# A decoder layer on one core: seven bodies with stops of their own, and constant waits on VectorE

## The chip, the core and the metric

One core of one Trainium2 chip. The engines are TensorE (PE; PEld is its weight load), VectorE (DVE), ScalarE (ACT), GpSimd (POOL) and SyncE (SP), which issues most DMAs. Time is the device time of one launch in microseconds (us); lower is better.

## What is computed

One layer of a decoder over 1024 tokens of width 1024, all in float32:

```python
x = x + hybrid_mixer(rmsnorm(x))            # MLA heads | gated linear recurrence | differential attention, then W_out
x = x + memory_cross_attention(rmsnorm(x))  # 256 memory rows, 4 heads
x = x + peer_ffn(rmsnorm(x))
return rmsnorm(x)

def peer_ffn(h):                            # 8 heads, 128 keys on each of two sides, 16 experts a head
    top_s, top_i = top_k(scores(h), 16)     # per side
    best_s, best_c = top_k(pairs_of(top_s), 16)
    experts = ...                           # 128 experts a token
    act = gelu(einsum('td,thkd->thk', h, u[experts]))
    return einsum('thk,thkd->td', softmax(best_s) * act, v[experts])
```

Each token needs 128 rows of `u` and 128 rows of `v`, 4 KB each, chosen by its own scores: 1.07 GB of gathered rows in all.

## The kernel before

The tokens are worked on in eight blocks of 128, one token to a partition. For a block the kernel has two kinds of work. The **rows**: 128 positions p, at each of which row p of `u` for every token is multiplied with the token's hidden vector and summed on VectorE (`multiply_row`, L2052), and a row of `v` is added to the result, thirteen positions later. Seven of eight `v` rows are summed on TensorE: ScalarE makes a diagonal matrix of the coefficients (L1528), and four matmul instructions add the row into PSUM (`add_row`, L1267). Each eighth is added on VectorE (L2074). The **front**: everything that leads from the block's x to its expert numbers and gates. Its pieces, in order, are `latents`, `mla_up`, `conv`, `gates`, `recur`, then attention (`mla_0` to `mla_3`, `diff_0` to `diff_3`, four heads each), `join`, `mix_out`, `norm_cross`, `cross_q`, `cross_scores`, `cross_mix`, `cross_out`, `norm_ffn`, `peer_q`, `peer_scores`, the top-16 searches (`top_0`, `choose_0`, `top_1`, `choose_1`), and, since the next block's first projection is drawn ahead, `next_square`, `next_norm`, `next_0` to `next_4`.

After an opening that prepares block 0 alone come seven **bodies**. Body n multiplies the rows of block n and runs the front of block n+1. A body is a loop that runs once, with its own number of key tiles for the attention (`LOOPS`: 2 in body 0 to 8 in body 6); body 6 has no next projection. At the end the rows of block 7 stand alone. The bodies' instruction streams are in order on each engine, and the order between rows and front is written out: `Pace.run` takes, for each piece of the front, a tuple of **stops** from the engine's table. A piece is cut into **parts** (`pace.part`), and before each part the engine first does all positions below the part's stop:

```python
            def part(self, share):

                self.to(int(self.first + share * (self.last - self.first)) if self.bp is None else next(self.ahead))
...
                        if self.bp is not None:
                            self.ahead = iter(self.stops[self.body][name])
```

So a part with stop 41 on TensorE starts when TensorE has been through positions 0 to 40. Parts with equal stops follow one another with no row between. TensorE, VectorE and ScalarE each have a table with one entry a body; all seven entries of a table are equal, but for the pieces that body 6 lacks. The parts wait for each other across engines by semaphores: a score matmul on TensorE (L1114, L1118), its masked maximum on VectorE (`masked_max`, L1834), the exponential on ScalarE (L1441), the transpose on TensorE in two halves (`turn_p`, L1100), between which ScalarE copies the first half out (`out_pT`), the values on TensorE (L1126).

GpSimd has no front. It issues the gathers (`retrieve`): one of `u`, one of `v`, in turn, 512 KB each, into two rings of nine rows. A `u` gather (L810) waits until VectorE has multiplied the row that held its slot; a `v` gather (L824) waits for the sum of the row that held its slot. `v` runs twelve rows behind `u`. SyncE loads weights in pairs of slices of 512 KB into a ring of four (`load_pair`); a pair is loaded when TensorE has used up the one four before. The weight pieces are `mix_out`, `cross_q`, `cross_out`, `peer_q` (eight pairs each) and `next_0` to `next_4` (17 pairs together).

VectorE counts three of its waits in registers: `wait_more` waits for a register's value plus n and then adds n to the register. It is used before each score maximum (twelve in a body), before each `top`, and between the steps of each top-16 search (`top16`): 32 times in a body.

## Time and profile before

| | us |
|---|---|
| median of 3 runs | 3484.84 |
| lowest and highest | 3477.87, 3487.18 |
| span of the profiled execution, first to last instruction (its own time; the page has no other) | 3488.4 |
| of it: opening, to the first row of body 0 | 306.6 |
| bodies 0 to 6, each from its first row product to the next body's | 384.3, 403.3, 401.5, 400.4, 413.2, 422.9, 412.2 |
| rows of block 7, end | 344.0 |

In the rows below, a window line gives the stretch in us from the span's start, its length, the busy time of each engine with the number of its instructions in brackets, the granted clock of TensorE as a share of full speed (2.4 GHz; the only other level is 1.2 GHz), the mean busy share of the 16 DMA engines, and the rate at which they moved data. A group line gives line, engine, operation, output and inputs, shapes and count, then busy time and the mean of one in ns, then the engine's idle time before it and what ended that. Busy time of TensorE is modelled from starts, since matmuls are pipelined.

### The profile page before, as it was taken

Reading aid. Unit: us, or ns where it says so; the run is one execution under the profiler, and the core shown is the slowest. Engines: PE = TensorE matmul, PEld = TensorE weight load, DVE = VectorE, ACT = ScalarE, POOL = GpSimd, SP = SyncE. Lnnn points to the kernel's source line nnn. Section 1 sums busy time; section 2 is a strip of 40 time slices with the busy share of each in tenths; the row PEclk is TensorE's granted clock in tenths of the full one; section 3 lists DMA queues with packets and bytes.
Section 4 is the critical chain, followed back from the end, with each engine's and each line's share of the span. In section 5 each row is a group of like instructions: output and inputs, shape, how many; then the busy total and the mean of one; then the engine's idle time right before and its main releaser. Section 6 shows DMA issues by size and latency. Waiting matters only on the chain.

```text
span 3488.4 us, 34790 instructions
## 1 busy us (share of the span) xinstructions
PE 2948.9 (85%) x10984; PEld 1651.9 (47%) x10984; DVE 2349.6 (67%) x5893; ACT 812.5 (23%) x1915; POOL 2015.7 (58%) x2085
## 2 busy tenths in 40 slices
PE   7876898888988898889997899888998889976675
PEld 6465455544545355534554456444564445522222
DVE  6229846886588765886578765886648865596555
ACT  3111411132211421133211322114221232211111
POOL 1004755666566765666565655665556655477775
PEclk9898999999999999999999999998999999999998
DMA  7788999999999999999999999999999999999998
GB/s 279 277 274 313 408 409 409 408 409 409 409 407 406 394 409 409 408 407 382 409 409 408 392 356 409 409 409 348 359 409 409 409 355 342 385 404 410 409 409 347
DMA packets 386971, 1345.09 MB, mean 386 GB/s; under 512 B 41762, under 2 KB 44834, under 8 KB 386148
## 3 DMA queue, kind: packets, MB, share of 16 engines
q0 software_dynamic: 294912, 1073.87, 78.1%
q1 hardware_dynamic: 90724, 264.79, 20.0%
q10 hardware_dynamic: 1152, 4.19, 0.3%
q8 instruction: 90, 1.47, 0.2%
q14 instruction: 93, 0.76, 0.1%
HBM read 1332.99 MB, written 35.39 MB: 392 GB/s over the span
## 4 chain that ended last, share of the span: by engine, by line
PE 38%; DMA 30%; DVE 15%; POOL 9%; issue 6%; ACT 3%; SPq 1%; DVEq 0%; POOLq 0%; ACTq 0%
PE ps_sum L1267 18%; DMA rows<-in_peer_u,ids_u 13%; DMA rows<-in_peer_v,ids_v 10%; PE ps_p L999 5%; POOL rows L824 5%; POOL rows L810 4%; DVE rows L2052 4%; PE ps_s L1181 4%; DMA rows<-in_peer_v,ids_u 3%; DMA w_ring<-packed 3%; PE ps_s L1118 2%; PE ps_p L1126 2%; DVE feat_b L1935 1%; DVE feat_b L1931 1%; PE ps_s L1114 1%
## 5 line engine op out<-in xcount | busy, mean ns | idle before, releaser
L1267 PE MATMUL ps_sum<-rows,diag 128*128 128x512 f32 x3548 | 1727.6, 629 | 267.1 <-DMA rows<-in_peer_v,ids_v 141.4
L2052 DVE CUSTOM_DVE_ANT_0 rows<-h_cur,rows 128x1024 f32<-128x1024 f32 x1024 | 1226.8, 1220 | 496.3 <-DMA rows<-in_peer_u,ids_u 483.3
L810 POOL DMA_INDIRECT rows<-in_peer_u,ids_u x1024 | 1012.3, 989 | 702.0 <-issue 483.3
L1267 PEld LDWEIGHTS ps_sum<-rows,diag 128*128 128x128 f32 x3548 | 671.0, 200 | 1155.7 <-issue 1005.7
L824 POOL DMA_INDIRECT rows<-in_peer_v,ids_v x512 | 490.3, 958 | 433.8 <-PE ps_sum L1267 277.6
L824 POOL DMA_INDIRECT rows<-in_peer_v,ids_u x512 | 498.2, 973 | 284.7 <-PE ps_sum L1267 144.2
L1528 ACT ACTIVATE diag<-ident,acts 128x128 f32<-128x128 f32 x887 | 324.7, 394 | 1049.4 <-PE ps_sum L1267 750.1
L999 PE MATMUL ps_p<-hT,w_ring 128*128 128x128 f32 x2944 | 358.7, 282 | 28.8 <-DMA w_ring<-packed 15.3
L999 PEld LDWEIGHTS ps_p<-hT,w_ring 128*128 128x128 f32 x2944 | 353.0, 198 | 61.2 <-issue 39.7
L1834 DVE CUSTOM_DVE_ANT_0 e<-ps_s,bias_t 128x256 f32<-128x256 f32 (+6 forms) x96 | 74.2, 773 | 176.3 <-PE ps_s L1118 73.7
L2074 DVE SCALAR_TENSOR_TENSOR x_cur<-rows,acts,x_cur 128x1024 f32<-128x1024 f32 x137 | 175.6, 1282 | 7.4 <-DMA rows<-in_peer_v,ids_v 7.3
L1905 DVE TENSOR_TENSOR x_next<-x_next,ps_s 128x512 f32<-128x512 f32 x32 | 21.9, 685 | 200.0 <-PE ps_s L1181 200.0
L1516 ACT ACTIVATE acts<-dots 128x8 f32<-128x8 f32 x128 | 26.6, 208 | 486.9 <-DVE dots L2052 486.6
L1181 PE MATMUL ps_s<-w_ring,hT 128*128 128x512 f32 x256 | 118.3, 608 | 14.2 <-DMA w_ring<-packed 7.4
L1441 ACT ACTIVATE e<-e,small 128x256 f32<-128x256 f32 (+6 forms) x96 | 75.4, 785 | 219.7 <-DVE small L1836 219.4
L999 PE MATMUL ps_p<-pT,w_ring 128*128 128x128 f32 x1024 | 118.8, 276 | 0.9 <-DMA w_ring<-packed 0.9
L999 PEld LDWEIGHTS ps_p<-pT,w_ring 128*128 128x128 f32 x1024 | 116.9, 192 | 5.4 <-issue 3.3
L1181 PE MATMUL ps_s<-w_ring,feat_b 128*128 128x512 f32 x256 | 114.8, 592 | 1.1 <-DMA w_ring<-in_wstream 1.1
L1935 DVE FIND_INDEX8 feat_b<-feat_b,e 128x8 uint32<-128x128 f32 (+1 forms) x384 | 103.4, 279 | 0.0
L1118 PE MATMUL ps_s<-k_diff,feat_a 32*128 32x512 f32 (+2 forms) x192 | 83.7, 543 | 16.9 <-DVE small L1836 16.8
L1314 ACT ACTIVATE feat_a<-ps_p 128x512 f32<-128x512 f32 (+2 forms) x48 | 26.0, 542 | 304.6 <-PE ps_p L999 304.5
L2052 DVE DVE_READ_ACCUMULATOR2_ANT dots<- 128x1 f32 x1024 | 84.4, 82 | 0.0
(288 smaller groups left out, 2376.2 us busy)
## 6 DMA issues: line engine op xcount, KB each, us to landing
w_ring<-packed SPq DMA_DIRECT2D x343, 512.0 KB
w_ring<-in_wstream SPq DMA_DIRECT2D x65, 512.0 KB
packed<-in_wstream SPq DMA_DIRECT2D x49, 512.0 KB, 8.2
rows<-in_peer_u,ids_u POOLq DMA_INDIRECT x1024, 14.9
rows<-in_peer_v,ids_u POOLq DMA_INDIRECT x512, 12.6
rows<-in_peer_v,ids_v POOLq DMA_INDIRECT x512, 19.3
bias_rows<-rows SPq DMA_DIRECT2D x5, 1024.0 KB, 12.1
bias_t<-in_x SPq DMA_DIRECT2D x8, 512.0 KB, 7.9
```

What stands on the lines that cost most here:

```text
L810: pool.indirect_dma_start(u_rows[:, slot, :], None, peer_u, bass.IndirectOffsetOnAxis(ap=ids_u[:, j:j + 1], axis=0)).then_inc(u_landed[slo ...
L824: pool.indirect_dma_start(v_rows[:, slot, :], None, peer_v, bass.IndirectOffsetOnAxis(ap=ids[:, j:j + 1], axis=0)).then_inc(v_landed[slot] ...
L999: ins = pe.matmul(dst, w[:, k, :], lhs[:, kt, :], start=(kt == 0), stop=(kt == KT - 1))
L1118: ins = pe.matmul(ps_s[:, c0:c1], q_diff[r:r + DK, half // 4, :], k_diff[r:r + DK, half // 4, c0:c1], start=True, stop=True)
L1181: pe.matmul(ps_s[:, n * 512:(n + 1) * 512], lhs[:, kt, :], w, start=(kt == 0), stop=(kt == KT - 1)).then_inc(w_used, 1)
L1267: ins = pe.matmul(ps_sum[:, c * 512:(c + 1) * 512], diag[:, n % 4, :], v_rows[:, slot, c * 512:(c + 1) * 512], start=(j == 0), stop=(n == ...
L1441: act.activation(buf[:, 0:keys_n], buf[:, 0:keys_n], ACT.Exp, bias=small[:, 32 + n:33 + n], accum_out=small[:, 48 + n:49 + n]).then_inc(s_ ...
L1528: act.activation(diag[:, n % 4, :], ident[:, :], ACT.Copy, scale=coef[:, j:j + 1]).then_inc(diag_made, 1)
L1834: run(dve.tensor_tensor_reduce(buf[:, 0:keys_n], ps_s[:, 0:keys_n], bias[:, 0:keys_n], 1.0, -3.0e38, ALU.add, ALU.max, small[:, 16 + n:17 ...
L1935: dve.max_index(i[:, first:first + 8], v[:, first:first + 8], s).then_inc(top_step, 1)
L2052: dve.tensor_tensor_reduce(row, h_cur[:, :], row, 1.0, 0.0, ALU.mult, ALU.add, dots[:, p:p + 1]).then_inc(u_used, 1)
L2074: dve.scalar_tensor_tensor(x_cur[:, :], v_rows[:, slot, :], coef[:, j:j + 1], x_cur[:, :], ALU.mult, ALU.add)\
```

## The change

Each of the seven entries of the three tables gets numbers of its own. `next_*` parts, `join`, attention, the searches and the rest keep their order; only the positions at which an engine turns to them differ. On VectorE the three counted waits no longer use registers: since each body runs once, the running count is known when the program is built, and `wait_for` waits for that constant. The waits, their number and their places are the same. SyncE's and GpSimd's programs don't change.

The diff, cut: of the old tables the entry that all bodies share; of TensorE's new one the lines for attention, join, `mix_out` and the end of each of bodies 0 to 6, body 6 in full; of VectorE's the lines of the searches, bodies 0 to 6 in order; of ScalarE's the entry of body 5.

```diff
 TENSOR_STOPS = [
-    {"latents": (1,), "mla_up": (9,), "gates": (17, 18), "recur": (20, 26), "mla_0": (29, 30, 31), "mla_1": (31, 31, 32),
-     "mla_2": (32, 33, 35), "mla_3": (35, 35, 37), "diff_0": (37, 38, 40, 41), "diff_1": (41, 43, 43, 44),
-     "diff_2": (45, 47, 48, 49), "diff_3": (49, 49, 51, 51), "join": (54, 56), "mix_out": (56, 56, 58, 58, 58),
-     "norm_cross": (59, 62), "cross_q": (62, 62, 62, 67, 67), "cross_scores": (69,), "cross_mix": (70, 73, 74),
-     "cross_out": (75, 75, 76, 78, 81), "norm_ffn": (83, 83), "peer_q": (83, 83, 85, 86, 88), "peer_scores": (89,),
-     "next_norm": (93, 99), "next_0": (104, 104, 106, 106), "next_1": (106, 106, 108, 108, 108),
-     "next_2": (112, 121, 121, 121, 121), "next_3": (121, 121, 124, 126, 126), "next_4": (126, 128, 128)},
...
+    {"latents": (8,), "mla_up": (16,), "gates": (19, 19), "recur": (23, 25), "mla_0": (27, 32, 32), "mla_1": (32, 32, 32),
+     "mla_2": (33, 33, 35), "mla_3": (35, 35, 35), "diff_0": (35, 40, 41, 41), "diff_1": (41, 42, 42, 42),
+     "diff_2": (42, 43, 47, 49), "diff_3": (49, 49, 49, 49), "join": (50, 53), "mix_out": (53, 59, 59, 63, 65),
...
+     "next_3": (108, 108, 108, 108, 108), "next_4": (108, 108, 114)},
+    {"latents": (4,), "mla_up": (12,), "gates": (18, 19), "recur": (19, 29), "mla_0": (32, 32, 32), "mla_1": (32, 33, 33),
+     "mla_2": (33, 34, 34), "mla_3": (34, 34, 34), "diff_0": (34, 42, 42, 42), "diff_1": (42, 43, 43, 44),
+     "diff_2": (48, 51, 51, 52), "diff_3": (52, 52, 52, 52), "join": (57, 62), "mix_out": (65, 65, 65, 65, 66),
...
+     "next_2": (104, 110, 110, 110, 110), "next_3": (110, 110, 110, 110, 114), "next_4": (114, 114, 114)},
+    {"latents": (0,), "mla_up": (1,), "gates": (7, 9), "recur": (22, 22), "mla_0": (24, 24, 26), "mla_1": (26, 26, 28),
+     "mla_2": (29, 30, 30), "mla_3": (30, 30, 31), "diff_0": (31, 33, 33, 36), "diff_1": (37, 42, 42, 42),
+     "diff_2": (43, 46, 46, 53), "diff_3": (53, 53, 53, 53), "join": (53, 56), "mix_out": (57, 57, 58, 58, 58),
...
+     "next_2": (107, 107, 107, 107, 108), "next_3": (108, 120, 120, 120, 120), "next_4": (120, 120, 120)},
+    {"latents": (3,), "mla_up": (4,), "gates": (8, 17), "recur": (24, 26), "mla_0": (28, 30, 31), "mla_1": (31, 31, 32),
+     "mla_2": (32, 34, 34), "mla_3": (37, 37, 37), "diff_0": (37, 41, 41, 41), "diff_1": (41, 44, 44, 44),
+     "diff_2": (46, 49, 49, 50), "diff_3": (50, 58, 58, 59), "join": (63, 63), "mix_out": (63, 63, 63, 63, 63),
...
+     "next_2": (105, 105, 105, 105, 108), "next_3": (110, 111, 111, 111, 111), "next_4": (111, 115, 115)},
+    {"latents": (3,), "mla_up": (3,), "gates": (7, 20), "recur": (22, 24), "mla_0": (29, 30, 30), "mla_1": (30, 31, 32),
+     "mla_2": (32, 32, 33), "mla_3": (33, 33, 35), "diff_0": (37, 38, 39, 40), "diff_1": (40, 42, 43, 43),
+     "diff_2": (45, 46, 49, 50), "diff_3": (50, 52, 62, 62), "join": (64, 65), "mix_out": (65, 65, 65, 66, 66),
...
+     "next_3": (108, 108, 108, 108, 108), "next_4": (108, 108, 108)},
+    {"latents": (3,), "mla_up": (9,), "gates": (19, 19), "recur": (19, 25), "mla_0": (28, 31, 31), "mla_1": (31, 32, 32),
+     "mla_2": (33, 34, 35), "mla_3": (35, 35, 38), "diff_0": (38, 39, 40, 41), "diff_1": (41, 43, 43, 44),
+     "diff_2": (44, 48, 48, 48), "diff_3": (48, 49, 51, 52), "join": (66, 66), "mix_out": (66, 66, 66, 66, 66),
...
+     "next_2": (104, 105, 105, 105, 105), "next_3": (109, 110, 111, 112, 112), "next_4": (112, 112, 113)},
+    {"latents": (2,), "mla_up": (2,), "gates": (7, 8), "recur": (8, 26), "mla_0": (28, 30, 30), "mla_1": (30, 31, 32),
+     "mla_2": (32, 33, 34), "mla_3": (34, 34, 38), "diff_0": (38, 39, 40, 41), "diff_1": (41, 43, 43, 44),
+     "diff_2": (45, 47, 48, 53), "diff_3": (53, 53, 57, 58), "join": (63, 64), "mix_out": (65, 65, 65, 65, 65),
+     "norm_cross": (66, 66), "cross_q": (67, 67, 67, 69, 70), "cross_scores": (71,), "cross_mix": (71, 79, 81),
+     "cross_out": (82, 83, 85, 85, 85), "norm_ffn": (88, 88), "peer_q": (90, 90, 90, 91, 92), "peer_scores": (92,)},
 ]
 VECTOR_STOPS = [
-    {"latents": (0, 6), "mla_up": (8,), "conv": (17,), "gates": (19, 19, 21, 23), "recur": (25, 26), "mla_0": (26,),
-     "mla_1": (29,), "mla_2": (33,), "mla_3": (39,), "diff_0": (39, 39, 39), "diff_1": (42, 42, 43), "diff_2": (43, 45, 48),
-     "diff_3": (50, 52, 52), "join": (53, 54), "mix_out": (54, 55, 57, 57), "norm_cross": (59, 59, 63), "cross_scores": (71,),
-     "cross_mix": (71, 72), "cross_out": (73, 76, 84, 84), "norm_ffn": (85, 85, 85), "next_square": (90, 93),
-     "top_0": (93, 94, 94, 94, 97, 99), "next_norm": (99, 103),
-     "choose_0": (104, 105, 105, 105, 106, 108, 108, 108, 108, 111, 111), "top_1": (113, 113, 113, 113, 114, 117),
-     "choose_1": (120, 120, 124, 125, 126, 126, 126, 128, 128, 128, 128)},
...
+     "top_0": (92, 92, 93, 94, 94, 97), "next_norm": (97, 97), "choose_0": (97, 97, 97, 97, 97, 98, 98, 99, 102, 107, 107),
+     "top_1": (107, 109, 109, 109, 109, 109), "choose_1": (109, 109, 109, 109, 111, 111, 115, 115, 116, 120, 121)},
...
+     "top_0": (95, 95, 95, 95, 95, 95), "next_norm": (95, 95), "choose_0": (95, 96, 96, 96, 97, 99, 99, 99, 111, 111, 112),
+     "top_1": (114, 114, 114, 114, 114, 114), "choose_1": (114, 114, 115, 115, 115, 115, 115, 115, 119, 119, 121)},
...
+     "top_0": (95, 96, 96, 96, 98, 100), "next_norm": (105, 105),
+     "choose_0": (105, 105, 105, 105, 105, 105, 106, 106, 106, 106, 106), "top_1": (106, 106, 106, 106, 106, 106),
+     "choose_1": (111, 121, 121, 121, 121, 121, 121, 121, 121, 121, 121)},
...
+     "top_0": (95, 98, 98, 98, 100, 101), "next_norm": (102, 102),
+     "choose_0": (105, 105, 105, 105, 105, 105, 105, 105, 105, 105, 106), "top_1": (112, 112, 112, 112, 112, 112),
+     "choose_1": (113, 114, 116, 116, 117, 117, 117, 119, 120, 127, 128)},
...
+     "top_0": (96, 97, 97, 97, 97, 97), "next_norm": (97, 97), "choose_0": (98, 98, 98, 99, 103, 103, 105, 105, 105, 105, 105),
+     "top_1": (105, 105, 105, 105, 109, 109), "choose_1": (109, 109, 109, 109, 109, 110, 114, 121, 121, 122, 123)},
...
+     "top_0": (91, 95, 99, 99, 99, 101), "next_norm": (102, 102),
+     "choose_0": (102, 102, 102, 102, 103, 103, 104, 104, 104, 109, 111), "top_1": (111, 111, 111, 111, 111, 111),
+     "choose_1": (111, 111, 111, 111, 112, 112, 112, 113, 113, 113, 117)},
...
+     "cross_mix": (77, 80), "cross_out": (80, 82, 86, 87), "norm_ffn": (87, 90, 90), "top_0": (93, 97, 97, 97, 97, 97),
+     "choose_0": (97, 103, 104, 104, 104, 104, 106, 108, 108, 110, 110), "top_1": (110, 110, 110, 112, 113, 113),
+     "choose_1": (113, 122, 127, 127, 127, 127, 127, 127, 128, 128, 128)},
 ]
 SCALAR_STOPS = [
-    {"latents": (1, 7), "mla_up": (10,), "gates": (14, 18, 20), "mla_0": (28, 30), "mla_1": (30, 30), "mla_2": (32, 32),
-     "mla_3": (32, 34), "diff_0": (34, 38, 42), "diff_1": (42, 42, 42), "diff_2": (47, 47, 48), "diff_3": (48, 51, 53),
-     "norm_cross": (59,), "cross_q": (59, 60, 67), "cross_scores": (71,), "cross_mix": (73, 73, 74), "norm_ffn": (82,),
-     "peer_q": (82, 84, 88), "next_square": (90,), "peer_scores": (90,), "next_0": (104, 109), "next_1": (114, 114),
-     "next_2": (117, 120), "next_4": (125, 125), "choose_1": (125, 125)},
...
+    {"latents": (4, 5), "mla_up": (6,), "gates": (6, 20, 20), "mla_0": (28, 30), "mla_1": (30, 30), "mla_2": (32, 32),
+     "mla_3": (32, 33), "diff_0": (36, 39, 40), "diff_1": (42, 43, 43), "diff_2": (44, 44, 47), "diff_3": (48, 50, 50),
+     "norm_cross": (71,), "cross_q": (71, 71, 71), "cross_scores": (72,), "cross_mix": (72, 72, 72), "norm_ffn": (86,),
+     "peer_q": (91, 91, 91), "next_square": (91,), "peer_scores": (91,), "next_0": (95, 100), "next_1": (101, 102),
+     "next_2": (104, 106), "next_4": (110, 111), "choose_1": (117, 117)},
...
 ]
             steps = Steps(dve_step)
-            scores_waited, keys_waited, top_waited = (counter(dve, n) for n in ("scores_waited", "keys_waited", "top_waited"))
+            scores_waited, keys_waited, top_waited = [0], [0], [0]
+
+            def wait_for(semaphore, waited, n):
+
+                waited[0] += n
+                dve.wait_ge(semaphore, waited[0])
...
-                wait_more(dve, s_ps, scores_waited, 1)
+                wait_for(s_ps, scores_waited, 1)
...
-                    wait_more(dve, top_step, top_waited, n)
+                    wait_for(top_step, top_waited, n)
...
-                    wait_more(dve, top_step, top_waited, 2 * n if first == 0 else n)
+                    wait_for(top_step, top_waited, 2 * n if first == 0 else n)
...
-                wait_more(dve, k_out, keys_waited, 1)
+                wait_for(k_out, keys_waited, 1)
...
-                wait_more(dve, top_step, top_waited, 2)
+                wait_for(top_step, top_waited, 2)
```

## Rows read from the trace of the kernel before

**Rows 1.** The page: span, busy time, DMA rate in 40 slices, totals.
```profile
span 3488.4 us, 34790 instructions
...
PE 2948.9 (85%) x10984; PEld 1651.9 (47%) x10984; DVE 2349.6 (67%) x5893; ACT 812.5 (23%) x1915; POOL 2015.7 (58%) x2085
...
GB/s 279 277 274 313 408 409 409 408 409 409 409 407 406 394 409 409 408 407 382 409 409 408 392 356 409 409 409 348 359 409 409 409 355 342 385 404 410 409 409 347
DMA packets 386971, 1345.09 MB, mean 386 GB/s; under 512 B 41762, under 2 KB 44834, under 8 KB 386148
```

**Rows 2.** Windows, one for each of bodies 1 to 6.
```profile
core 0: us, PE busy (x) PEld busy (x) DVE busy (x) ACT busy (x) POOL busy (x), PEclk, DMA share, GB/s
...
690.90:1094.20 403.30, 351.73 (x1300) 197.04 (x1300) 284.00 (x725) 97.42 (x238) 250.28 (x257) 0.94 1.03 408
1094.20:1495.70 401.50, 352.39 (x1324) 195.94 (x1324) 286.39 (x724) 99.47 (x238) 250.53 (x256) 0.96 1.02 405
1495.70:1896.10 400.40, 353.14 (x1374) 200.87 (x1372) 288.05 (x725) 102.54 (x238) 251.44 (x257) 0.98 1.02 403
1896.10:2309.30 413.20, 365.00 (x1396) 206.72 (x1396) 290.14 (x724) 104.75 (x238) 250.36 (x257) 0.96 1.00 394
2309.30:2732.20 422.90, 376.44 (x1420) 212.79 (x1420) 292.60 (x725) 107.00 (x238) 253.09 (x257) 0.94 0.99 386
2732.20:3144.40 412.20, 350.58 (x1176) 183.15 (x1176) 290.55 (x711) 105.34 (x230) 246.71 (x255) 0.96 0.97 377
```

**Rows 3.** Windows of the attention stage, bodies 1 to 6.
```profile
762.70:830.40 67.70, 58.13 (x178) 27.96 (x177) 50.03 (x115) 27.63 (x71) 50.11 (x52) 0.92 1.03 408
1163.40:1234.20 70.80, 62.58 (x202) 29.85 (x201) 51.67 (x113) 29.75 (x71) 48.80 (x51) 0.95 1.00 390
1565.10:1640.20 75.10, 66.02 (x250) 36.10 (x249) 53.81 (x114) 32.89 (x71) 51.25 (x52) 1.00 1.01 390
1967.90:2052.60 84.70, 74.51 (x274) 40.66 (x273) 55.84 (x113) 34.91 (x71) 51.59 (x52) 0.96 0.96 361
2379.90:2478.10 98.20, 87.70 (x298) 47.32 (x297) 58.09 (x113) 37.07 (x71) 53.61 (x53) 0.88 0.89 326
2804.50:2902.00 97.50, 84.60 (x322) 46.40 (x321) 60.26 (x113) 38.94 (x71) 50.85 (x52) 0.97 0.92 337
```

**Rows 4.** Groups by line in body 5's attention stage: busy, mean ns, idle before.
```profile
L824 POOL DMA_INDIRECT rows<-in_peer_v,ids_u x26 | 24.9, 958 | 30.9 <-PE ps_sum L1267 23.9 <-issue 7.0
...
L1100 PE MATMUL ps_p<-ident,e 128*128 128x128 f32 x56 | 10.3, 304 | 8.4 <-ACT pT L1314 7.7 <-DVE e L1867 0.7
```

**Rows 5.** Timeline of GpSimd in body 6: start, duration, idle before and its releaser.
```profile
3046.66 0.94 POOL L824 DMA_INDIRECT rows<-in_peer_v,ids_v  x1 [9.25 <-PE ps_sum L1267]
3047.90 0.94 POOL L810 DMA_INDIRECT rows<-in_peer_u,ids_u  x1 [0.30 <-DVE dots L2052]
```

**Rows 6.** Window: the first slow part of body 5's attention stage.
```profile
2400.00:2412.00 12.00, 11.85 (x29) 6.61 (x27) 4.36 (x9) 4.08 (x7) 3.13 (x4) 0.54 0.78 292
```

**Rows 7.** Groups by line in body 5's weight stage: the row sums.
```profile
L1267 PE MATMUL ps_sum<-rows,diag 128*128 128x512 f32 x253 | 119.4, 616 | 9.9 <-DMA rows<-in_peer_v,ids_v 8.9 <-ACT diag L1528 1.0
```

**Rows 8.** Window of that stage, mix_out to next_4.
```profile
2484.80:2727.00 242.20, 220.76 (x949) 134.57 (x947) 160.68 (x443) 39.68 (x101) 144.47 (x150) 0.97 1.02 406
```

**Rows 9.** DMA issues in that stage: weight pairs, count, size of one.
```profile
w_ring<-packed SPq DMA_DIRECT2D x48, 512.0 KB
```

**Rows 10.** Window in body 2: choose_0 and top_1.
```profile
1405.00:1457.30 52.30, 42.07 (x173) 23.89 (x172) 45.38 (x152) 6.58 (x20) 35.45 (x37) 0.97 1.03 409
```

**Rows 11.** Groups by line in that window: products of U rows.
```profile
L2052 DVE CUSTOM_DVE_ANT_0 rows<-h_cur,rows 128x1024 f32<-128x1024 f32 x17 | 20.4, 1220 | 6.2 <-DMA rows<-in_peer_u,ids_u 5.6 <-DVE feat_b L1935 0.2 <-DVE e L1937 0.2
```

**Rows 12.** Window in body 6 after peer_scores.
```profile
3036.00:3064.00 28.00, 25.41 (x59) 11.23 (x58) 22.25 (x85) 7.04 (x15) 14.68 (x15) 0.94 0.85 316
```

**Rows 13.** Timeline of VectorE in body 6 at the start of top_0.
```profile
3037.87 1.64 DVE L1931 MAX8 feat_b<-e 128x8 f32<-128x128 f32 x8
3039.64 0.09 DVE L1935 MATCH_VALUE_LOAD feat_b<-feat_b,e 128x8 f32 x1
```

137 lines of the change are left out of this document (59 added, 78 removed), and 47 rows, old and new, of tables (SCALAR_STOPS, VECTOR_STOPS).

## Prediction, made before the changed kernel was run

> **What bounds the kernel now.** I read the page first. Over the 3488.4 us span TensorE is busy 85%, VectorE 67%, GpSimd 58%, and the DMA rate per slice stands at 409 GB/s in most slices and never above 410 [rows 1]. 1345.09 MB at 409 GB/s would take 3289 us, so the queues are the floor, and what a schedule can win is only the time in which they run below 409. The table of windows by body says where that is [rows 2]: a body's duration times (1 - rate/409) is 1.0 us in body 1, 3.9 in body 2, 5.9 in body 3, 15.2 in body 4, 23.8 in body 5, 32.3 in body 6, 82 us together. (Body n multiplies the rows of token block n and prepares block n+1.)
>
> The windows of the attention stage alone, from `mla_0` to the end of `diff_3`, show the cause [rows 3]. In all bodies the old table gives this stage stops 29 to 51, 22 positions, but it lasts 67.7 us in body 1 and 98 in bodies 5 and 6, since each body has one key tile more. A position brings two rows of 512 KB: 1.05 MB / 409 = 2.56 us of DMA, 56.3 us for 22 positions. What the stage takes beyond that is TensorE's lag: 11.4, 14.5, 18.8, 28.4, 41.9, 41.2 us in bodies 1 to 6. In the lines of body 5's stage GpSimd sits 30.9 us idle before its V gathers, 23.9 of it ended by TensorE's row sums [rows 4]. So the chain is: late sums, no free V slot, no gather, idle DMA. Against the losses above (body 6 without the 6.4 us treated below) the lag that costs nothing is 10.4, 10.6, 12.9, 13.2, 18.1, 15.3 us. I take a **cover** of 14, bounds 10 and 18: that is what the nine slots of each ring have in flight. GpSimd can't build it up again quickly, since it issues one gather every 1.24 us, 2.49 per position [rows 5], hardly faster than the DMA's 2.56.
>
> TensorE is really full there (87.7 of 98.2 us busy in body 5), and the rest is mostly its wait for ScalarE's copy between the two halves of a transpose, 7.7 us [rows 4], which stands inside a part and no stop can move. Body 5 has one thing more: its stage ran at a granted clock of 0.88 against 0.97 in body 6 [rows 3], with 12 us at 0.54, nearly all at the 1.2 GHz level [rows 6].
>
> **The change, part by part.** No arithmetic is added or removed, no DMA is moved in SyncE's or GpSimd's own order; what moves is when TensorE, VectorE and ScalarE leave the rows for a part of the next block. Three stages matter.
>
> *Attention.* One position more in the stage costs TensorE a row sum, 119.4 us for 253 instructions [rows 7], four to a row and seven rows in eight: 1.65 us. It gives the DMA 2.56. So each added position takes 0.91 off the lag.
> - Body 2 goes from 22 to 29 positions (24 to 53): lag 14.5 - 6.4 = 8.1, under the cover: saves 3.9.
> - Body 3 does the last head's transpose and values at 58. At 50 the lag is 18.8 less about 4 for these: 14.8, saves 4.
> - Body 4 puts them at 62, with 21 positions before: 28.4 - 4 + 0.9 = 25.3, saves 3.
> - Body 5 keeps its stage (28 to 52): saves 1.8. The slow clock can fall elsewhere: 0.09 of 98.2 is 9 us, so 0 to 9; with 2 of it I take 4.
> - Body 6 stretches to 30 positions: 41.2 - 7.3 = 33.9, saves 7.
> - Body 1 packs all four MLA heads into positions 32 to 34. TensorE's waits there are 67.7 - 58.1 = 9.6 us [rows 3]; with no rows between them they could double. Bounds 0 and 9.6; I take 5, since heads still overlap by one score. Lag 11.4 + 1.8 + 5 = 18, some 4 above the cover, 3.5 more than now. Body 0 does the same with a smaller tile: 1.
>
> *Weights, `mix_out` to `next_4`.* Old stops 56 to 128. New: 53-114, 65-114, 57-120, 63-115, 65-108, 66-113 in bodies 0 to 5, thus 61, 49, 63, 52, 43, 47 positions instead of 72. In body 5 this stage runs at 406 GB/s and loses 2 us [rows 8]. TensorE is busy 220.8 us, of it 119.4 rows [rows 7], so 101.4 for the front; of its 21.4 idle 8.9 waits for rows, 12.5 for others. The 48 loads of 512 KB [rows 9] take 1.28 each, 61.4 us. The lag for n positions is 101.4 + 12.5 + 1.65n - 2.56n - 61.4 = 52.5 - 0.91n: at 72 it is -13, in the new bodies -3, 8, -5, 5, 13, 10. All stay under 14: cost 0, and 3 in body 4 at a cover of 10; I take 1. So moving join and `mix_out` ten positions back is paid from slack that the stage had.
>
> *Top and choose on VectorE.* The new table heaps them up. In body 2 all of `choose_0` and `top_1` stands at 105 and 106. In the window where the old kernel does these two, VectorE is busy 45.4 us [rows 10], of it 20.4 products of 17 rows [rows 11] and 2.6 additions: 22 us, 24 with `next_norm`, in two positions. Less 2.3 of DMA time that the two rows give, 22 of lag; eleven weight loads (14 us) start at TensorE's stop 107 and feed the queues meanwhile: 8 to 22, I take 15. Parts at one stop and the next, counted in the same way less the loads that start there, give 14, 14, 9, 13, 14, 14 in bodies 0, 1, 3, 4, 5, 6. With the cover of 14 this costs 1, with 10.4 it costs 22; since three bodies showed 10 to 13, I take 5.
>
> *Body 6 after `peer_scores`.* GpSimd waited 9.25 us for a row sum [rows 5] and the stretch ran at 316 GB/s, 6.4 us lost [rows 12]. New: `peer_q` and `peer_scores` packed into 90-92, so that eight loads feed the queues just before. Between 0 and 6.4; I take half, 3.
>
> *Counted waits.* 32 in a body stand on a register that is then added to. Between the last of eight MAX8 and the next load lie 0.13 us [rows 13]: 3039.64 - (3037.87 + 1.64). A wait can't give more. VectorE has room everywhere but in the twelve score maxima of a body, where TensorE may wait for it: 12 x 7 x 0.13 = 11 at most, 0 at least. TensorE's wait is elsewhere in the costly bodies, so 2.
>
> Sum: -3.9 - 4 - 3 - 4 - 7 - 3 - 2 = -26.9, and +3.5 + 1 + 1 + 5 = +10.5; net -16.4. The profiled execution's span is 3488.4, 3.6 above the median of the runs, 3484.84; so 3472.0 on the span, **3468** as runs are timed.
>
> **Rivals.** (a) *No change, about 3484.* TensorE's work in the attention stage is the same, and the slow clock comes along: what body 5 shows (0.88) need only reach bodies 4 and 6 (0.96 and 0.97), 0.08 x 84.7 + 0.09 x 97.5 = 15.6 us. For it: the new parts stand closer, and TensorE waits for ScalarE and VectorE between them without a row to sum. Against: the bodies 4 and 6 had such waits too and kept 0.96. The Trainium skill, "TensorE: Matmul & The Clock Gate", section "HAM oscillation — how this bites in real kernels", has it as a rule that a TensorE which idles in bursts falls back to half rate and starts the next burst slow; it speaks against packed parts. The trace agrees with it for one body of six only [rows 3, 6].
>
> (b) *Slower, about 3507.* VectorE's heaps are not covered. If the cover for U rows is 7 instead of 14, they cost 44 instead of 5: 3468 + 39. At 10.4 they take back all that the rest wins; below about 8.7 the kernel is over 0.3% slower. For it: GpSimd's speed, hardly above the DMA's, and the 6.4 us in body 6, where a 9 us wait was enough for a loss. Against: that loss came after weight loads had ended; in bodies 0 to 5 loads run beside the heaps.
>
> (c) *More, about 3445.* All at their good ends: the clock's 9, the 6.4, 11 for the waits, no heap: about 40. More is hardly there: bodies 4 and 5 keep their attention stops.
>
> That the tables don't act is excluded: each body reads its own already, with equal contents.
>
> **How the numbers follow.** 0.3% (10.5 us) is about what a measurement of this kernel can tell from no change. Forecast and (c) are faster: 0.48 and 0.10. (a), with sums that end within 10 us of no change: 0.26. (b): 0.16. The likeliest case's own bounds are 3450 and 3476. The range takes in (a) and half of the way from there to (b), and most of (c): 3442 to 3497.
>
> **What would show it.** Right: windows by body with body 6 down by about 10 us, bodies 2 to 4 by 3 to 5 each, body 5 still the worst attention stage (below 350 GB/s); the weight stages at 406 or more. Wrong: a rate under 395 in positions 92 to 121 with GpSimd waiting for VectorE's products (b); attention stages of bodies 4 and 6 at a clock under 0.9 (a); body 5's loss gone although its stops are the same, which would mean that the order on ScalarE and VectorE, not TensorE's load, set it.

## The result, and the profile after

The changed kernel takes 3557.64 us (median of 4 runs, 3555.14 to 3559.81) against 3483.91 for the kernel before on the same chip: ratio 1.0215, 95% interval 1.0197 to 1.0233. It is 2.15% slower, on the other side of no change than the forecast, and outside its range.

The windows of bodies 1 to 6 of the changed kernel, which answer to [rows 2]:

```profile
core 0: us, PE busy (x) PEld busy (x) DVE busy (x) ACT busy (x) POOL busy (x), PEclk, DMA share, GB/s
694.20:1114.70 420.50, 358.36 (x1307) 199.34 (x1306) 290.59 (x741) 98.27 (x239) 255.09 (x263) 0.93 1.01 394
1114.70:1527.40 412.70, 359.06 (x1318) 200.08 (x1318) 280.81 (x709) 99.70 (x237) 243.36 (x250) 0.94 0.99 387
1527.40:1951.20 423.80, 371.39 (x1376) 209.04 (x1376) 287.43 (x724) 104.04 (x238) 251.79 (x256) 0.94 0.99 387
1951.20:2367.60 416.40, 367.95 (x1393) 209.71 (x1392) 289.08 (x723) 105.21 (x238) 244.21 (x249) 0.94 0.99 388
2367.60:2797.20 429.60, 377.87 (x1421) 212.00 (x1420) 292.16 (x723) 107.22 (x239) 258.12 (x264) 0.94 0.98 383
2797.20:3213.20 416.00, 361.02 (x1177) 187.04 (x1176) 290.39 (x712) 105.58 (x230) 255.80 (x261) 0.92 0.97 376
```

Bodies 1 to 5 lost rate, bodies 1 to 3 most: they had 403 to 408 GB/s and are now at 387 to 394. Body 6 stands at 376, where it had 377. The windows of the attention stage, which answer to [rows 3]:

```profile
779.20:853.10 73.90, 61.51 (x170) 29.37 (x169) 46.75 (x107) 27.35 (x69) 45.83 (x50) 0.85 0.95 356
1180.40:1267.10 86.70, 72.72 (x222) 35.35 (x221) 58.77 (x125) 32.80 (x78) 61.15 (x63) 0.90 1.01 396
1601.50:1702.80 101.30, 90.44 (x278) 46.30 (x277) 61.09 (x128) 36.99 (x79) 66.32 (x68) 0.88 0.96 365
2025.40:2126.70 101.30, 90.63 (x310) 47.29 (x309) 68.38 (x136) 39.72 (x82) 67.50 (x70) 0.97 0.99 383
2440.60:2538.40 97.80, 88.47 (x302) 47.29 (x301) 61.23 (x119) 39.19 (x75) 58.44 (x59) 0.90 0.89 336
2876.40:2985.00 108.60, 100.22 (x346) 52.79 (x345) 71.98 (x135) 42.35 (x78) 66.66 (x69) 0.92 0.95 358
```

Bodies 4 and 6 gained there (361 to 383 and 337 to 358 GB/s), body 5 hardly (326 to 336), bodies 1 and 3 lost (408 to 356, 390 to 365). The granted clock fell in bodies 1, 2, 3 and 6.

To see the rest, I took from the packet records of each trace the duration of every 16 positions less the time that the bytes moved in it take at 409.5 GB/s, and summed this loss over bodies 0 to 6 (us; e1_waits is the old tables with constant waits, the other rows are explained below):

| positions | 0-31 | 32-63 | 64-79 | 80-95 | 96-111 | 112-127 | sum |
|---|---|---|---|---|---|---|---|
| before | 11 | 74 | 1 | 2 | 5 | 1 | 94 |
| e1_waits | 11 | 65 | 0 | 2 | 6 | 2 | 87 |
| after | 34 | 62 | 10 | 19 | 36 | 4 | 164 |
| e2_early | 47 | 54 | 0 | 1 | 3 | 2 | 107 |
| e7_attention | 17 | 83 | 0 | 0 | 4 | 1 | 106 |
| e4_weights_top | 11 | 51 | 12 | 17 | 34 | 3 | 128 |
| e13_short_tail | 9 | 53 | 15 | 39 | 1 | 5 | 121 |
| e10_stretch_b4_b6 | 14 | 40 | 0 | 2 | 4 | 2 | 62 |

From before to after the loss account grew by 70 us, the span by 67: it is all idle queue. What was lost before stood in the attention; the new losses stand ahead of it and, most of all, behind it. In the column 32-63 the ten traces whose stops up to `diff_3` are the old ones range from 51 to 74, so there only a larger difference says something.

A site in body 2, GpSimd's timeline first, then TensorE's (start, duration, count, idle before and its releaser), then windows:

```profile
1296.52 0.94 POOL L821 DMA_INDIRECT rows<-in_peer_v,ids_u  x1 [12.59 <-PE ps_sum L1264]
...
1312.71 0.94 POOL L807 DMA_INDIRECT rows<-in_peer_u,ids_u  x1 [0.31 <-issue]
1329.86 0.94 POOL L821 DMA_INDIRECT rows<-in_peer_v,ids_u  x1 [16.21 <-PE ps_sum L1264]
```

```profile
1308.83 7.31 PE L996 MATMUL ps_p<-pT,w_ring 128*128 128x128 f32 x64
1317.64 2.05 PE L996 MATMUL ps_p<-pT,w_ring 128*128 128x128 f32 x16 [1.50 <-DMA w_ring<-packed]
1321.41 2.05 PE L996 MATMUL ps_p<-pT,w_ring 128*128 128x128 f32 x16 [1.72 <-DMA w_ring<-packed]
1324.15 3.72 PE L1202 MATMUL ps_s<-mem_k,feat_a 128*128 128x256 f32 x16 [0.69 <-ACT feat_a L1311]
```

```profile
1324.00:1328.00 4.00, 3.85 (x17) 3.34 (x18) 1.27 (x3) 0.10 (x1) 0.00 (x0) 1.00 1.03 410
1328.00:1332.00 4.00, 4.00 (x10) 1.71 (x9) 2.50 (x4) 0.80 (x2) 1.83 (x2) 1.00 0.32 80
1332.00:1336.00 4.00, 4.00 (x11) 1.84 (x10) 0.17 (x1) 0.90 (x3) 2.85 (x4) 1.00 0.89 339
1336.00:1340.00 4.00, 4.00 (x11) 1.77 (x10) 1.97 (x3) 0.81 (x3) 3.01 (x4) 1.00 0.88 319
1340.00:1344.00 4.00, 4.00 (x10) 1.71 (x9) 1.99 (x5) 2.71 (x6) 3.08 (x4) 1.00 0.96 375
1344.00:1348.00 4.00, 3.88 (x10) 1.63 (x9) 2.17 (x3) 3.42 (x11) 3.08 (x4) 1.00 1.02 416
```

TensorE does the last three parts of `cross_q` and `cross_scores` at one stop (18.9 us, no row sum), GpSimd gets no V slot for 16.21 us, the queues run on what they hold and on the weight loads until 1328 and are then nearly empty (80 GB/s). Over bodies 0 to 6 GpSimd's waits that end on TensorE's row sums add up to 414 us in e1_waits and 566 in the changed kernel; those that end on VectorE's products fall from 207 to 135. Gathers also stand in the queues for less time. The page's rows of DMA issues (count, median us from issue to landing) for the old tables (e1_waits), then for the changed kernel:

```profile
rows<-in_peer_u,ids_u POOLq DMA_INDIRECT x1024, 15.0
rows<-in_peer_v,ids_u POOLq DMA_INDIRECT x512, 12.5
rows<-in_peer_v,ids_v POOLq DMA_INDIRECT x512, 18.9
```

```profile
rows<-in_peer_u,ids_u POOLq DMA_INDIRECT x1024, 8.6
rows<-in_peer_v,ids_u POOLq DMA_INDIRECT x512, 8.0
rows<-in_peer_v,ids_v POOLq DMA_INDIRECT x512, 10.0
```

15.0, 12.5 and 18.9 us have become 8.6, 8.0 and 10.0: over the whole kernel a third to a half of what used to stand in the queues is gone.

### The profile page after: what moved, and what is told of

It is laid out like the page before. It is cut to its first block, busy times and chain, and to the rows that moved or that the text cites. A ratio compares the mean times of both kernels' runs of the same rounds, so it can differ in the third digit from the quotient of the medians.

```text
span 3555.3 us, 34336 instructions
## 1 busy us (share of the span) xinstructions
PE 3003.8 (84%) x10984; PEld 1679.7 (47%) x10984; DVE 2349.4 (66%) x5893; ACT 816.8 (23%) x1915; POOL 2017.0 (57%) x2085
## 4 chain that ended last, share of the span: by engine, by line
PE 47%; DVE 18%; DMA 17%; POOL 9%; issue 5%; ACT 4%; SPq 0%; DVEq 0%; POOLq 0%; ACTq 0%
PE ps_sum L1264 22%; DMA w_ring<-packed 8%; PE ps_p L996 6%; DVE rows L2054 5%; DMA rows<-in_peer_u,ids_u 5%; POOL rows L821 5%; PE ps_s L1178 5%; POOL rows L807 4%; DMA rows<-in_peer_v,ids_v 3%; PE ps_s L1115 2%; PE ps_p L1123 2%; DVE feat_b L1937 2%; DVE feat_b L1933 1%; PE ps_p L1097 1%; DMA rows<-in_peer_v,ids_u 1%
## 5 line engine op out<-in xcount | busy, mean ns | idle before, releaser
L807 POOL DMA_INDIRECT rows<-in_peer_u,ids_u x1024 | 999.4, 976 | 634.7 <-issue 497.0
L1264 PEld LDWEIGHTS ps_sum<-rows,diag 128*128 128x128 f32 x3548 | 683.0, 201 | 1137.4 <-issue 996.8
L821 POOL DMA_INDIRECT rows<-in_peer_v,ids_v x512 | 505.6, 988 | 506.7 <-PE ps_sum L1264 364.0
L1178 PE MATMUL ps_s<-w_ring,hT 128*128 128x512 f32 x256 | 126.1, 638 | 15.7 <-DMA w_ring<-packed 11.8
L996 PE MATMUL ps_p<-pT,w_ring 128*128 128x128 f32 x1024 | 122.6, 277 | 12.7 <-DMA w_ring<-packed 11.8
L1097 PE MATMUL ps_p<-ident,e 128*128 128x128 f32 x256 | 48.7, 293 | 48.2 <-ACT pT L1311 26.4
L1311 ACT ACTIVATE pT<-ps_p 128x512 f32<-128x512 f32 (+2 forms) x112 | 52.1, 472 | 162.2 <-PE ps_p L1097 136.2
```

Of the source, the lines that this page charges most:

```text
L807: pool.indirect_dma_start(u_rows[:, slot, :], None, peer_u, bass.IndirectOffsetOnAxis(ap=ids_u[:, j:j + 1], axis=0)).then_inc(u_landed[slo ...
L821: pool.indirect_dma_start(v_rows[:, slot, :], None, peer_v, bass.IndirectOffsetOnAxis(ap=ids[:, j:j + 1], axis=0)).then_inc(v_landed[slot] ...
L996: ins = pe.matmul(dst, w[:, k, :], lhs[:, kt, :], start=(kt == 0), stop=(kt == KT - 1))
L1097: ins = pe.transpose(bank[:, (t - t0) * P:(t - t0 + 1) * P], src[:, t * P:(t + 1) * P], ident[:, :])
L1178: pe.matmul(ps_s[:, n * 512:(n + 1) * 512], lhs[:, kt, :], w, start=(kt == 0), stop=(kt == KT - 1)).then_inc(w_used, 1)
L1264: ins = pe.matmul(ps_sum[:, c * 512:(c + 1) * 512], diag[:, n % 4, :], v_rows[:, slot, c * 512:(c + 1) * 512], start=(j == 0), stop=(n == ...
```

## The experiments

All have the constant waits. Differences are against e1_waits, as differences of the two ratios to the kernel before; 0.1% is 3.5 us. A heap is a run of front parts at one stop or at neighbouring stops. Theory A, at the start: a heap on TensorE stops the row sums, and each heap pays for itself. Rivals: VectorE's heaps (B), the waits (R).

**One part of the change at a time.**

e1_waits:
```diff
-                wait_more(dve, s_ps, scores_waited, 1)
+                wait_for(s_ps, scores_waited, 1)
...
 (tables as before)
```


> All three tables as before, only VectorE's counted waits stand on constants. Loss is meant as the time in which the queues move less than 409.5 GB/s. Theory A (heaps on TensorE: while it does several front parts in a row it sums no rows, no V slot comes free, GpSimd's gathers stop, and the queues run empty): the waits have no part in the 73 us, so 3484, within 5 us, 454 instructions fewer. Rival R (the constant waits changed when VectorE's score maxima start, and with it the order of everything behind): the loss comes with the waits alone, 3530 or more.

3479.93, ratio 0.9985 (0.9972 to 0.9999). The waits gain 5 us, by the interval 0 to 10; R is out.

e2_early:
```diff
-"latents": (1,), "mla_up": (9,), "gates": (17, 18), "recur": (20, 26)
+"latents": (0,), "mla_up": (1,), "gates": (7, 9), "recur": (22, 22)
...
 (body 2 on TensorE; the new stops of these pieces in all bodies on all three engines)
```


> Constant waits, and the new stops for latents, mla_up, conv, gates and recur alone, on all three engines; the rest as before. In the traces of before and after the first 32 positions lose 11 us before and 34 after. Theory A: about +20 us, in the first 16 positions of bodies 2, 3, 4 and 6, with GpSimd waiting for row sums; about 3505. Rival B (the heaps on VectorE, choose and top, empty the queues and the bodies start empty for that reason): under +5 us, since choose and top stand as before.

3512.23, ratio 1.0085 (1.0055 to 1.0114): +35, where A said 20. Its runs spread from 3503.94 to 3518.48, and the profiled one is the fastest: its bodies are 20 us longer than those of e1_waits, with 36 us more lost at positions 0 to 31 and 11 less at 32 to 63. Body 2's worst place, TensorE's timeline, then GpSimd's, then windows:

```profile
1085.88 3.73 PE L1015 MATMUL ps_p<-w_ring,hT 128*128 128x128 f32 x32
1094.91 0.80 PE L1054 MATMUL ps_s<-pT,ones 128*128 128x128 f32 x2 [5.30 <-DVE pT L1756]
...
1103.44 0.79 PE L1063 MATMUL ps_p<-feat_a,wuq 128*128 128x128 f32 x2 [2.87 <-DVE feat_a L1766]
```

```profile
1120.60 0.94 POOL L821 DMA_INDIRECT rows<-in_peer_v,ids_v  x1 [14.87 <-PE ps_sum L1264]
```

```profile
1083.00:1094.50 11.50, 6.62 (x40) 4.75 (x38) 10.37 (x16) 4.72 (x9) 5.74 (x7) 1.00 1.03 408
1094.50:1121.90 27.40, 23.60 (x47) 12.09 (x48) 20.88 (x53) 3.43 (x8) 3.00 (x4) 0.50 0.68 269
```

`latents` now follows the last projection with no row between. TensorE waits 5.30 us for VectorE; from 1094.5 on it is granted 0.50, the 1.2 GHz level, for 27.4 us, and the pieces take twice as long: in e1_waits the same L1063 groups take 0.38 to 0.49 us, here 0.79. No weight load runs beside them. The Trainium skill, "TensorE: Matmul & The Clock Gate", section "HAM oscillation — how this bites in real kernels", says that a TensorE that waits long enough between bursts starts the next one at half rate; this site agrees, 5.30 us of idling and then 27.4 us at 0.50.

A first form of the next experiment, e3_early_att, took the early and the attention stops together and left what stands behind them at its old stops. It has no time: its engines wait for each other in a circle.

e7_attention:
```diff
-"mla_0": (29, 30, 31), ... "diff_3": (49, 49, 51, 51), "join": (54, 56), ... "next_4": (126, 128, 128)
+"mla_0": (24, 24, 26), ... "diff_3": (53, 53, 53, 53), "join": (55, 57), ... "next_4": (126, 128, 128)
...
 (body 2 on TensorE; likewise all bodies and engines)
```


> The early stops as before, the new attention stops (mla_0 to diff_3) on all three engines, and behind them the old stops, spread over what is left of the body (old 51 to 128 onto the new end of diff_3 to 128, the same for the three engines), so that no new heap arises there. By the prediction's terms for this stage, -3.9, -4, -3, -4 and -7 in bodies 2 to 6 and +4.5 in bodies 0 and 1: 3480 - 17 = 3463. By the traces, before with constant waits against after (positions 32 to 63: bodies 1 and 3 lose 12 more, bodies 4 to 6 19 less): about 3470. If stretching gives nothing: 3480 or more.

3496.58, ratio 1.0035 (1.002 to 1.005): +17, where the prediction's terms give -17. By body (first row product to the next, against e1_waits): 0, +2.1, +11.8, +13.5, +1.3, +5.4, -11.4 us. Body 6, which was stretched most, gained more than the 7 of the forecast; bodies 2 and 3 lost where a gain of 4 was forecast for each, and bodies 4 and 5, forecast at -3 and -4, gained nothing. The timeline of body 2 begins with a gap of 16.5 us between row sums, since two heads of MLA stand at 24 to 26, in it this wait, and then matmuls at half rate (2.08 us for what took 1.02 at 1157.33):

```profile
1157.33 1.02 PE L1111 MATMUL ps_s<-k_lines,feat_b 96*128 96x512 f32 x2
1164.20 2.08 PE L1111 MATMUL ps_s<-k_lines,feat_b 96*128 96x512 f32 x2 [5.85 <-DVE small L1838]
```

e4_weights_top:
```diff
-"join": (54, 56), "mix_out": (56, 56, 58, 58, 58), ... "next_0": (104, 104, 106, 106)
+"join": (50, 53), "mix_out": (53, 59, 59, 63, 65), ... "next_0": (96, 96, 96, 96)
...
 (body 0 on TensorE; from join on the new stops in all bodies and engines)
```


> The old stops up to diff_3, the new ones from join on, on all three engines, choose and top too. The slices from position 64 on lose 7 us before and 68 after. Theory A: +61 with the attention as before, about 3545, lost in positions 64 to 120 of all bodies, GpSimd's waits there ended by TensorE's row sums. Rival B: the same sum but GpSimd's waits ended by VectorE's products, in positions 97 to 114 only.

3521.95, ratio 1.0105 (1.0079 to 1.013): +42, where A said 61. GpSimd's waits at its loss sites end nearly all on TensorE's row sums; VectorE's products end the longest one at a single site, body 2's positions 105 to 114, as in the changed kernel (14.76 us). The three groups give +35, +17 and +42, 94 us; all together, 80. They don't simply add: at positions 32 to 63 e7_attention loses 83 us and the changed kernel, with the same attention stops, 62.

**Heaps alone.**

e5_three_heaps:
```diff
-"mix_out": (56, 56, 58, 58, 58), "cross_q": (62, 62, 62, 67, 67), "peer_q": (83, 83, 85, 86, 88)
+"mix_out": (56, 56, 56, 56, 56), "cross_q": (62, 62, 62, 62, 62), "peer_q": (83, 83, 83, 83, 83)
```


> The old tables (with the constant waits, which by themselves gave 3480), but on TensorE alone mix_out goes to stop 56, cross_q to 62 and peer_q to 83 with all five parts, in every body: three heaps of eight weight pairs each, no stop on VectorE or ScalarE touched, no stage made longer or shorter. Theory A (a heap stops the row sums, and what the queues still hold and the loads of the heap are used up before the gathers return): such heaps of 18 to 19 us cost 0 to 5 us in the trace after, so 21 of them about 50, range 25 to 90, GpSimd waiting for row sums at positions 57 to 93. Rival S (the prediction's own sum: the lag of the whole stage counts, the loads feed the queues within it): under 10 us. Rival B (VectorE's heaps are the cause): under 5.

3503.03, ratio 1.006 (1.004 to 1.008): +26, at the lower end of A's range; S and B are out. But the 21 heaps, all 19 to 21 us, don't cost alike: up to 15 us behind their end those of `mix_out` lose nothing in bodies 0 to 2 and 4 to 5 us in 3 to 6, behind the longer attention stages; those of `cross_q` 0 to 3; those of `peer_q` 0 to 1.5, but 6.4 in body 6.

e6_next_heap:
```diff
-"next_2": (112, 121, 121, 121, 121), "next_3": (121, 121, 124, 126, 126), "next_4": (126, 128, 128)
+"next_2": (121, 121, 121, 121, 121), "next_3": (121, 121, 121, 121, 121), "next_4": (121, 121, 121)
```


> As e5_three_heaps, but the one heap is at the end of the body: next_2 to next_4 all at TensorE's stop 121 in bodies 0 to 5 (it was 121 to 128, with a gap of 11 to 13 us between row sums and no loss). Theory A: gaps of 22 us or more, 3 to 6 us in each of six bodies, about +25. Rivals S and B: 0.

3478.21, ratio 0.9984 (0.9971 to 0.9996): 0. The gaps in the row sums are 24 to 26 us, longer than those of e5_three_heaps; up to 15 us behind their end they cost under 0.5 in four bodies and about 4 in bodies 1 and 2. A, which gave 3 to 6 in each, falls: the length of a heap doesn't decide. Twelve loads of 1.28 us fit into this one, which leaves 9 to 10 us of lag, under the cover of 14.

e12_one_heap:
```diff
-"cross_q": (62, 62, 62, 67, 67)
+"cross_q": (62, 62, 62, 62, 62)
```


> Of the three heaps of e5_three_heaps only the one of cross_q at stop 62, on TensorE alone, in all seven bodies (constant waits, old tables). In e5 the row sums stood still 19 us for it, six positions behind the 20 us heap of mix_out, and the slices of positions 64 to 79 lost 0, 2.4, 1.6, 2.2, 2.4, 2.3, 2.8 us in bodies 0 to 6, while the same heap of peer_q, 22 positions further on, lost 0.1 to 1.6. Theory D (TensorE's backlog runs on from heap to heap and is worked off by only 0.91 us a position; a loss comes where the running backlog, not a heap or the mean of a stage, passes the cover): with no heap ahead of it it loses next to nothing, under 4 in all: 3480 to 3484. Theory A (each heap pays for itself): about 14, 3494.

3484.28, ratio 1.0000 (0.999 to 1.0011): +5, at the upper end of D, far from A. Positions 64 to 79 lose 8 us here and 14 in e5_three_heaps: there the same heap costs nearly twice as much with another ahead of it.

e8_early_and_next_heap:
```diff
 (the stops of e2_early and the heap of e6_next_heap)
```


> The early stops of e2_early (3512) and the heap of e6_next_heap (3478, so nothing by itself) together. Theory C (one reserve: what stands in the queues between GpSimd's issue and landing is used up by a heap and comes back only while loads run beside a GpSimd that is free; in e1_waits a mean of 12 to 13 rows is in flight at the start of a body, in e6_next_heap 7 to 8): the early heap that follows meets 5 rows less, 5 x 1.28 = 6 us more in each body whose early heap already lost (2, 3, 4 and 6): about 3530, range 3520 to 3540. Theory A as it stood and the prediction's sum (each heap against a cover of its own): the two add, 3510.

3507.42, ratio 1.0075 (1.0056 to 1.0094): +31, no more than e2_early alone. Theory C falls: rows in flight are not the whole stock. A V slot that is free counts too, since GpSimd can still fill it while TensorE is away (at the early heap of body 4 it waited 21.0 us in e2_early and 12.4 here, and the slices lost 10 and 12). That fits Theory D, by which it matters how far TensorE is behind and not how full the queue is.

e9_choose_heap:
```diff
-"choose_0": (104, 105, 105, 105, 106, 108, 108, 108, 108, 111, 111), "top_1": (113, 113, 113, 113, 114, 117)
+"choose_0": (106,) * 11, "top_1": (107,) * 6
```


> The old tables with constant waits, but on VectorE alone choose_0 goes to 106 with all eleven parts and top_1 to 107 with all six, in all seven bodies: the heap of body 2 of the changed kernel, seven times. Prediction: 22 us of lag less 2 to 14 against a cover of 14, 0 to 5 a body, about +5 in all: 3485. Theory C: the stretch has 8 to 12 rows in flight before the heap, 10 to 15 us, and the loads of next_0 and next_1 beside it: 0 to 3 a body, 3480 to 3500. Rival B (cover of 7): 8 to 13 a body, 3535 or more.

3485.76, ratio 1.0008 (0.9994 to 1.0022): +8. B is out. The prediction's price for VectorE's heap, 0 to 5 a body, is near: from position 96 on the trace loses 23 us, against 8 in e1_waits, 4 and 3 of the difference in bodies 1 and 2 and 6 in body 6.

**The length of the stage alone.**

e13_short_tail:
```diff
-"join": (54, 56), "mix_out": (56, 56, 58, 58, 58), ... "next_4": (126, 128, 128)
+"join": (61, 62), "mix_out": (62, 62, 64, 64, 64), ... "next_4": (111, 113, 113)
```


> Everything up to diff_3 as before; from join on the old stops of all three engines pressed together evenly, from 52-128 onto 60-113, in all seven bodies: mix_out to next_4 in 51 positions instead of 72, as short as in the changed kernel (43 to 63 positions), but in the old proportions. Prediction's sum for the stage: lag 52.5 - 0.91 x 51 = 6, under the cover: nothing lost. Theory D: the same as long as no heaps meet: 3480 to 3490, so that the +42 of e4_weights_top came from how its parts are bunched. Rival P (the stage needs its positions: too few rows beside the weights): as e4_weights_top, 3515 or more.

3511.66, ratio 1.0077 (1.006 to 1.0094): +32, close to P, and D, as it was put, is wrong: no heap was added, and yet three quarters of what e4_weights_top costs is there, though at other places, nearly all at positions 64 to 95. The prediction's sum for the stage is refuted with it. At the loss site of body 1, GpSimd's timeline and the window:

```profile
979.23 0.94 POOL L821 DMA_INDIRECT rows<-in_peer_v,ids_v  x1 [7.16 <-PE ps_sum L1264]
```

```profile
976.00:990.00 14.00, 14.00 (x36) 6.37 (x35) 13.89 (x74) 3.54 (x8) 8.34 (x9) 1.00 0.97 355
```

e14_short_first_half and e15_short_second_half:
```diff
-"join": (54, 56), ... "peer_scores": (89,), "next_norm": (93, 99), ... "next_4": (126, 128, 128)
+"join": (61, 62), ... "peer_scores": (86,), "next_norm": (93, 99), ... "next_4": (126, 128, 128)
```
```diff
-"peer_scores": (89,), "next_norm": (93, 99), "next_0": (104, 104, 106, 106), ... "next_4": (126, 128, 128)
+"peer_scores": (89,), "next_norm": (91, 95), "next_0": (98, 98, 99, 99), ... "next_4": (111, 113, 113)
```


> Of the pressed tail of e13_short_tail (3512) only its first half: join to peer_scores of all bodies from 52-90 onto 60-87, what stands behind as before. In e13 the losses stand at positions 75 to 81 and 88 to 92, that is behind cross_out and peer_q, and none behind position 96. Theory D (what counts is the running backlog, so the densest piece of a stage): 27 positions instead of 38 for 32 of the 48 loads, all of the +32 is here: 3505 to 3515. Rival P (the mean over the whole stage: 51 positions are too few): about half, 3495.

> The other half alone: everything up to position 90 as before, what stands from 90 to 128 (top, choose, next_norm to next_4) pressed onto 90 to 113 on all three engines. Theory D: GpSimd has its ring full after peer_scores and twelve positions with hardly any front are ahead: 3478 to 3488, no stretch that loses more than 1 us in bodies 0 to 5. Rival P: about half of the +32, 3495. Rival B (VectorE's choose and top, pressed from 25 into 15 positions): losses at positions 95 to 113 that end on VectorE's products, 3490 or more.

3496.84, ratio 1.0033 (1.0019 to 1.0048), +17; and 3485.83, ratio 1.0014 (1.0002 to 1.0027), +10, of which 7 stand at the end of body 6. In bodies 0 to 5 the second half loses nothing over 0.5 in any 16 positions from 80 on, the first half 0 to 6 in positions 80 to 95 (and 12 in body 6). The dense first half is what costs most, though less than D's 25 to 35; P, which gave 3495 for each half, is right for the first and not for the second.

**The same reasoning used for a faster kernel.**

e10_stretch_b4_b6, e11_stretch_b3_b6 and e16_hole_b5_b6:
```diff
-"mla_0": (29, 30, 31), ... "diff_3": (49, 49, 51, 51), "join": (54, 56), ... "next_4": (126, 128, 128)
+"mla_0": (28, 30, 30), ... "diff_3": (53, 53, 57, 58), "join": (60, 62), ... "next_4": (126, 128, 128)
...
 (bodies 4 to 6; e11: 3 to 6; e16: in 5 and 6 diff_2 and diff_3 eight later, what follows onto 66 to 128)
```


> Constant waits; bodies 0 to 3 as before; in bodies 4, 5 and 6 the early stops as before, the new attention stops of body 6 (28 to 58) in all three, and behind them the old stops spread from 51-128 onto 58-128. In e7_attention body 6 went from 411.7 to 400.3 us with these. Theory C: the stage starts with its full reserve (9 to 10 rows in flight) and has 8 positions more, 0.91 each: bodies 4, 5 and 6 lose 12 + 9 + 8 us less, less what the body behind 58 gives back: 3455, range 3448 to 3465. Rival (body 6 gained only because it alone has nothing to load after position 92): only body 6 gains, 3468.

> As e10_stretch_b4_b6, with body 3 too. Body 3 lost 6 us in e1_waits with the old stops and 16 in e7_attention with its own new ones. Theory C: body 3 has the least work there and gains at most its 6 us: 0 to -6 against e10_stretch_b4_b6, 3450. If it is the shape of body 6's stops that costs in body 3 (four score matmuls of mla_1 to mla_3 at 30 to 34): up to +8.

> e10_stretch_b4_b6 (3453) with eight positions more between diff_1 and diff_2 in bodies 5 and 6, where 10 and 14 us are still lost between positions 32 and 54, and the tail behind spread from 51-128 onto 66-128. Theory D: 8 x 0.91 = 7 us less backlog for the second half of the stage in each, less 1 to 4 for the tail that is eight positions shorter: 3443 to 3453. If the loss sits ahead of diff_2 (the first half of the stage is as dense as before): 3453 to 3458.

3453.18, ratio 0.9914 (0.9897 to 0.9931): faster than both kernels. 3452.87 (0.9885 to 0.993) and 3452.87 (0.9889 to 0.9938): neither adds anything. Windows of bodies 4, 5 and 6 of e1_waits, then of e10_stretch_b4_b6:

```profile
1894.10:2302.10 408.00, 364.38 (x1397) 208.35 (x1396) 290.38 (x724) 104.82 (x238) 248.76 (x256) 0.96 1.01 398
2302.10:2720.50 418.40, 371.07 (x1421) 210.79 (x1420) 292.10 (x725) 106.87 (x238) 248.57 (x257) 0.96 1.00 393
2720.50:3132.20 411.70, 358.02 (x1176) 185.60 (x1176) 290.42 (x711) 105.35 (x230) 246.86 (x253) 0.94 0.97 376
```

```profile
1892.60:2295.30 402.70, 363.62 (x1397) 206.69 (x1396) 289.47 (x725) 105.36 (x238) 247.10 (x256) 0.96 1.02 405
2295.30:2709.60 414.30, 374.18 (x1421) 212.46 (x1420) 292.48 (x725) 107.52 (x238) 246.48 (x257) 0.95 1.01 397
2709.60:3109.40 399.80, 347.76 (x1176) 179.91 (x1176) 289.11 (x712) 105.64 (x230) 247.13 (x255) 0.97 1.00 388
```

All three bodies are shorter, body 6 by 12 us, and nothing is given back behind position 64: the rival, that only body 6 could gain, falls. `mix_out` to `next_4` in 66 positions instead of 72 is free, where 51 are not. In e16 body 6 gained 5 in the attention and lost 4 at positions 96 to 111.

## Why the prediction was wrong, step by step

**"Three stages matter."** The first step that failed. Positions 0 to 31 were left out, that is put at nothing; their stops alone cost +35 by the runs of e2_early (20 by its trace), and in the changed kernel these positions lose 34 us where e1_waits loses 11. The diff shows `latents` at 0 to 3 with `mla_up` beside it in four bodies, and these parts have no weight load.

**Attention, -17.** Wrong by 35 us. The term 0.91 us for an added position holds where the work is spread with the positions: e10_stretch_b4_b6 gave bodies 4, 5 and 6 eight positions, 7.3 us by that term, and took 7, 6 and 12 us off their loss at positions 32 to 63 (body 6 loses 3 more just ahead of them). But the lag was taken as a mean over the stage. Body 2's seven added positions stand at its end, behind four MLA heads at 24 to 31; the loss begins there (e7_attention: 3, 7 and 6 us in its slices from 16 to 63), which fits a running lag that passes the cover first at that place. "They could double" for TensorE's waits in packed heads was written for body 1 alone; in the changed kernel's windows TensorE's idle time in the stage went from 9.6 to 12.4 us in body 1, from 8.2 to 14.0 in body 2 and from 9.1 to 10.9 in body 3.

**Weights, 0 to 1.** Wrong by some 40 us (e4_weights_top, +42). The step that failed is the mean over the stage: 52.5 - 0.91 n joins a dense half and a loose one. e13_short_tail, at 6 by this formula and so free, lost 32, and e14_short_first_half 17 with the dense half alone. The first half alone in body 1 of e1_waits, join to peer_scores, window and the group of row sums:

```profile
836.20:971.40 135.20, 124.05 (x527) 76.34 (x528) 61.66 (x120) 25.75 (x61) 68.22 (x73) 0.99 1.03 409
```

```profile
L1264 PE MATMUL ps_sum<-rows,diag 128*128 128x512 f32 x119 | 54.2, 594 | 1.9 <-DMA rows<-in_peer_v,ids_u 1.9
```

Front: 124.05 - 54.2 = 69.9, and 135.2 - 124.05 - 1.9 = 9.3 of waits, less 32 loads of 1.28: lag 38.2 - 0.91 n. That is 8 for the 33 positions of the old table (`mix_out` 56 to `peer_scores` 89), 14 for 27 (65 to 92, the changed bodies 1 and 6) and 16 for 24 (body 5, and 62 to 86 in e14_short_first_half). So the prediction's own formula, taken for the dense half, comes to the cover where the mean stayed below it. It gives no sizes, though: at 16 in every body, e14_short_first_half lost 0 to 7 us in bodies 0 to 5, most in bodies 1 and 2, and bodies 0, 2, 3 and 4 of the changed kernel (30 to 37 positions, 5 to 11 by the formula) lost 2 to 7 at positions 64 to 95. And 40 of the 69 us that the changed kernel loses from position 64 on stand behind 96, past this half. "The weight stages at 406 or more" was wrong: body 5's runs at 391 from `mix_out` to the last loads [rows 8].

```profile
2560.00:2760.00 200.00, 179.58 (x843) 117.58 (x843) 121.82 (x381) 32.21 (x76) 101.00 (x106) 0.96 1.00 391
```

**Heaps on VectorE, 5.** Right in size (e9_choose_heap, +8). **Waits, -2.** Right in sign and size (-5, 0 to -10 by the interval). **peer_scores, -3.** Not gained: positions 80 to 111 of body 6 lost 6 before and 10 after.

**The cover of 14.** It stands as an order of size: 25 us of heap less 15 of loads cost nothing in four bodies of six and 4 in two (e6_next_heap), 16 to 21 us without loads cost 4 to 12 (e2_early, bodies 2, 3, 4 and 6). What failed is that each stage was set against a full cover of its own. TensorE works its backlog off by 0.91 us a position, an estimate from the 2.56 and 1.65 us of the prediction, so two dense stretches close together share one cover; e5_three_heaps against e12_one_heap shows that for heaps six positions apart. The prediction said that GpSimd can't build the stock up again quickly, and did not use it.

**What would show it.** Body 5 kept the worst attention stage, at 336 GB/s as foretold; body 6, to be 10 us shorter, is 4 longer, and bodies 2 to 4, to be 3 to 5 shorter, are 11, 23 and 3 longer [rows 2]. The low rates in positions 92 to 121 come with GpSimd waiting for row sums, a sign that no rival had; only in body 2 does the longest wait show the sign of (b) (14.76 us).

**The rivals.** (b) had the sign and the sign alone: the waits that grew end on TensorE's row sums (414 to 566 us), not on VectorE's products (207 to 135), and a cover of 7 is excluded by e9_choose_heap, which should then have come to 3535 or more. (a) had a true mechanism, the slow clock behind a wait with no row to sum, but as a reason for no change, and in bodies 4 and 6. That the trace agreed "for one body of six only" was read too narrowly: the slow clock had a part in the stage of body 1 too, at 0.92 [rows 3]. Summed over bodies 0 to 6, the trace has TensorE at the 1.2 GHz level for 273 us in e1_waits, 284 in e4_weights_top, 335 in both e2_early and e7_attention, 382 after. So the clock bears on the early and the attention stops and hardly on the weights.

**Open.** How much of the early +35 and of the attention's +17 is the clock and how much the missing row sums: 62 us more at half rate is at most 31 of TensorE's work, and a kernel that keeps TensorE busy through those waits was not tried. In e4_weights_top 34 us are lost at positions 96 to 111, and in the changed kernel 36, where the evenly pressed e13_short_tail and e15_short_second_half lose 1 and 5. In bodies 0 to 5 of e4_weights_top, with 23 of the 34, it fits that the new heaps of `next_0` to `next_3` meet a backlog there, but that was not shown by itself; in body 2 the wait ends on VectorE. The other 10 stand in body 6, which has no `next` parts: there GpSimd waits 10.6 us for a row sum at position 97, as it did before the change (10.3 in e1_waits, with 6 lost). So the largest single loss of the change is placed, not explained.

## What to carry to other kernels

In a stream written in order against a ring of buffers, a stage's mean slack can mislead (here 0 to 1 us forecast, 42 measured): add up the running backlog part by part, carry it into the next stage, and look for where it first passes what the ring holds. Take the sum as a place to look and not as a size: put as Theory D, it was right for e12_one_heap and e15_short_second_half and missed e13_short_tail and e14_short_first_half. A part moved next to the one that it waits for can lose twice, once for the rows that no longer fill the wait and once for the clock that falls in it (e2_early, body 2). Count every place that a diff moves, above all those that cost nothing today.

## What the runs showed of the hardware

- Queues that had run nearly empty took some 12 us to come back to full rate: in body 2 of the changed kernel GpSimd issued 512 KB each 1.24 us from 1329.86 on, which is 423 GB/s, and the stretches of 4 us from 1332 on ran at 339, 319, 375 and then 416 GB/s.
- 5.3 us of idling on TensorE were followed by 27.4 us at 0.50 (e2_early, body 2).
- In a heap, once the ring of four loads was used up, TensorE got a load only every 2.56 us, though the queues move one in 1.28: gathers and loads share them, 2.45 and 2.44 MB from 1276 to 1288 at 409 GB/s together. In e5_three_heaps, body 2:

```profile
1280.58 2.05 PE L996 MATMUL ps_p<-pT,w_ring 128*128 128x128 f32 x16 [0.51 <-DMA w_ring<-packed]
1283.14 2.05 PE L996 MATMUL ps_p<-pT,w_ring 128*128 128x128 f32 x16 [0.51 <-DMA w_ring<-packed]
1285.70 2.05 PE L996 MATMUL ps_p<-pT,w_ring 128*128 128x128 f32 x16 [0.51 <-DMA w_ring<-packed]
```
